# Attention in two places of a two-layer block: each pair's transpose is issued one iteration after its scores, where it was two

## The chip, the cores and the metric

The kernel runs on one core of a Trainium2 chip. The metric is the device time of one execution in microseconds (us). The kernel before was timed in three executions.

## The reference, cut to what matters

The reference runs a first layer (a Hyena mixer and a differential attention mixer) and then a second layer with a mixer and a mixture of experts. The change concerns only the second layer's mixer, which holds two attentions over 512 positions in blocks of 128 queries, all in float32:

```
def dsa_attention(q, k, v, qi, ki, wi):          # 8 heads, one shared key and value
    score = einsum('bth,bths->bts', wi, relu(einsum('bthd,bsd->bths', qi, ki)))
    _, sel = lax.top_k(where(causal, score, -inf), k_sel)     # 128 keys of each query
    s = einsum('bthd,btkd->bthk', q, k[sel]) * scale
    out = einsum('bthk,btkd->bthd', masked_softmax(s, sel <= qpos), v[sel])

def nsa_attention(...):                          # 8 heads in 2 groups
    o_cmp = attention over compressed keys       # blocks of 32 positions
    o_slc = attention over selected blocks       # softmax(q k^T) v
    o_win = attention over a window
    o = gc * o_cmp + gs * o_slc + gw * o_win     # gates per query and head

merged = sigmoid(gate_a) * (o_a @ w_br_a) + sigmoid(gate_b) * (o_b @ w_br_b)
```

The kernel computes the whole causal score row and masks it, so the work of a query block i (0 to 3) is over 128*(i+1) keys.

## The kernel before, in words

The program is written by hand, one instruction list for each engine, with semaphores between them: `tensor`, `scalar`, `vector`, `gpsimd` and `sync` each call their part of each stage in the same order of stages. An engine works its own list strictly in the written order. Nothing but that order decides what stands behind what.

Attention is cut into *pairs*, numbered in the table `PAIRS` (L2869). A pair is one query block with two heads, r = 0 and 1. Pairs 0 to 15 are the first attention, called DSA here (kind "a": query blocks 0 to 3, four pairs each). Pairs 16 to 47 are the second, called NSA here (kinds "slc" and "win", eight pairs for each query block). A *quad* c is the pairs 2c and 2c+1, whose products with the values are made together. The steps of a pair n are:

- `tensor_scores` on TensorE: six matmuls (L3007, L3008) and two that add a mask (L3015), into one of two sets of PSUM banks.
- `vector_scores` on VectorE: two maxima over a row (L3023).
- `scalar_scores` on ScalarE: two exponentials with their row sums (L114), into the buffers R and X of the pair's parity.
- `vector_weigh` on VectorE: the reciprocal of the sums (L3050). For NSA it also multiplies by the gates (L3055) and scales both tiles (L119). For DSA `scalar_weigh` scales them on ScalarE (L114).
- `tensor_turn` on TensorE: i+1 transposes (L3085) for each r, into banks 4 and 5. It waits for the scaled tile and for the previous pair's reads of these banks.
- `scalar_turn` on ScalarE: the high part of the transposed tile (`hi_part`, L98). `vector_turn` on VectorE: the low part (`lo_part`, L102). Both go to tiles called pt_a0h, pt_a0l and so on.
- `tensor_product` on TensorE, once for each quad: 6*(i+1) matmuls (L92 to L94) with the values. For "slc" quads `tensor_compressed_out` adds six matmuls twice. `vector_out` copies the result out (L3145) for all but the "slc" quads, whose result goes on in the same bank.

Between the steps of pair n each engine calls `between(n)`. On TensorE this is `tensor_gate`: matmuls of the projections for `gate_a` and `gate_b`, which need nothing of the attention. They are 12 matmuls of 512 columns for each pair of DSA and 6 for each pair of NSA. On ScalarE it is the conversion of weight chunks (`whi`, L98) and the eviction of the gate results (`gslot`, L114); on GpSimd the gate result is multiplied (L2959); on VectorE it is the low part of weight chunks (`wlo`, L102) and, in DSA, three rounds of `vector_choose` for each pair (L2731, L2733), the selection of the 128 keys, until all are found. The first `between` of NSA (n = 16) also ends the compressed attention's last block (`cT_last`), and `tensor_turn(16)` waits for it.

Each engine's loop is one of the functions `tensor_attend`, `scalar_attend` and `vector_attend`. In the kernel before they have three stages: in iteration n the engine works on the scores of pair n, on the scaling of pair n-1 and on the transpose of pair n-2. The product of a quad stands at the end of the odd iteration n = 2c+3.

## Time and profile before

| | us |
|---|---|
| median of 3 executions | 2574.6 |
| lowest and highest | 2572.97, 2575.89 |
| profiled execution: its own time | 2575.89 |
| profiled execution: span of the trace | 2574.1 |
| PE busy (matmuls) | 2363.1 (92%) |
| DVE busy (VectorE) | 1676.8 (65%) |
| ACT busy (ScalarE) | 1305.7 (51%) |
| POOL busy (GpSimd) | 800.1 (31%) |

The span is the time from the first to the last instruction in the trace; the profiled execution's own time is 1.8 us longer. PE is TensorE's matmuls, PEld its weight loads, DVE is VectorE, ACT is ScalarE, POOL is GpSimd. Matmuls overlap each other, so that a row of a matmul shows a longer time than the step to the next one: steps are read from start to start. Of the span, DSA is the stretch from 1655.7 to 1762.2 us and NSA the stretch from 1855.8 to 2018.7 us. In the profile's 40 slices these are roughly slices 26 to 28 and 29 to 32.

### The profile page before, as it was taken

Reading aid. Unit: us, or ns where it says so; the run is one execution under the profiler, and the core shown is the slowest. Engines: PE = TensorE matmul, PEld = TensorE weight load, DVE = VectorE, ACT = ScalarE, POOL = GpSimd, SP = SyncE. Lnnn points to the kernel's source line nnn. Section 1 sums busy time; section 2 is a strip of 40 time slices with the busy share of each in tenths; the row PEclk is TensorE's granted clock in tenths of the full one; section 3 lists DMA queues with packets and bytes.
Section 4 is the critical chain, followed back from the end, with each engine's and each line's share of the span. In section 5 each row is a group of like instructions: output and inputs, shape, how many; then the busy total and the mean of one; then the engine's idle time right before and its main releaser. Section 6 shows DMA issues by size and latency. Waiting matters only on the chain.

```text
span 2574.1 us, 38547 instructions
## 1 busy us (share of the span) xinstructions
PE 2363.1 (92%) x15891; PEld 2092.4 (81%) x15891; DVE 1676.8 (65%) x2609; ACT 1305.7 (51%) x2147; POOL 800.1 (31%) x496
## 2 busy tenths in 40 slices
PE   8999996989899899999999898888898996999997
PEld 7999996888899889988998677667776775878875
DVE  4454545878843766666656667884576546888885
ACT  4444433444432555555555534354254325888885
POOL 2112123454531122232232022122210023776773
PEclk9999997999999999999999899998898997999999
DMA  5333321011043122222222142123211434878874
GB/s 177 92 90 99 117 62 50 18 33 34 13 134 87 47 78 73 81 67 71 71 75 58 50 110 82 54 54 100 82 50 29 135 109 173 293 279 294 285 263 172
DMA packets 226056, 272.88 MB, mean 106 GB/s; under 512 B 41544, under 2 KB 194089, under 8 KB 213210
## 3 DMA queue, kind: packets, MB, share of 16 engines
q1 hardware_dynamic: 211626, 262.00, 32.6%
q0 software_dynamic: 14256, 8.44, 1.1%
q8 instruction: 125, 2.05, 0.3%
q14 instruction: 49, 0.40, 0.1%
HBM read 282.74 MB, written 31.00 MB: 122 GB/s over the span
## 4 chain that ended last, share of the span: by engine, by line
PE 57%; DVE 20%; ACT 10%; POOL 6%; issue 5%; DMA 2%; SPq 0%; DVEq 0%; POOLq 0%; ACTq 0%
PE ps L92 17%; PE ps L93 16%; PE ps L94 16%; ACT whi L98 2%; DVE wlo L102 2%; DVE prods L1163 2%; PE ps L1839 2%; DVE fsum L990 1%; ACT sp L114 1%; POOL wlo L102 1%; DVE p L2134 1%; POOL xg L3987 1%; PE ps L1849 1%; DVE work L2733 1%; POOL yd L3993 1%
## 5 line engine op out<-in xcount | busy, mean ns | idle before, releaser
L92 PE MATMUL ps<-hn_h,whi 128*128 128x264 f32 (+2 forms) x2256 | 689.9, 306 | 23.7 <-POOL wlo L102 10.3
L94 PE MATMUL ps<-hn_h,wlo 128*128 128x264 f32 (+2 forms) x2256 | 670.1, 297 | 0.0
L93 PE MATMUL ps<-hn_l,whi 128*128 128x264 f32 (+2 forms) x2256 | 670.0, 297 | 0.0
L92 PEld LDWEIGHTS ps<-hn_h,whi 128*128 128x128 f32 x2256 | 428.9, 190 | 52.9 <-issue 17.1
L94 PEld LDWEIGHTS ps<-hn_h,wlo 128*128 128x128 f32 x2256 | 427.9, 190 | 11.6
L93 PEld LDWEIGHTS ps<-hn_l,whi 128*128 128x128 f32 x2256 | 429.7, 190 | 8.9 <-issue 0.2
L102 POOL TENSOR_TENSOR wlo<-wraw,whi 128x2048 fp32r<-128x2048 f32 (+1 forms) x45 | 163.1, 3624 | 540.6 <-ACT whi L98 540.6
L98 ACT ACTIVATE whi<-wraw 128x2048 fp32r<-128x2048 f32 (+1 forms) x164 | 260.4, 1588 | 52.7 <-PE ps L94 44.1
L102 DVE TENSOR_TENSOR wlo<-wraw,whi 128x2048 fp32r<-128x2048 f32 (+1 forms) x119 | 247.2, 2077 | 54.4 <-ACT whi L98 54.3
L750 DVE SCALAR_TENSOR_TENSOR c<-ub,vec,c 128x528 f32<-128x528 f32 x48 | 45.6, 950 | 128.5 <-ACT c L114 128.5
L114 ACT ACTIVATE ub<-ps,vec 128x528 f32<-128x528 f32 x48 | 33.7, 702 | 151.3 <-PE ps L94 151.3
L2184 POOL TENSOR_TENSOR sp<-sp,sp 128x512 f32<-128x512 f32 x16 | 23.5, 1469 | 237.4 <-DMA sp<-sp 237.4
L114 ACT ACTIVATE p<-ps,stat 128x528 f32<-128x528 f32 x64 | 45.0, 703 | 98.3 <-DVE stat L2120 98.2
L3993 POOL DMA_INDIRECT yd<-ys,dst x39 | 84.0, 2153 | 17.2 <-issue 7.7
L3987 POOL DMA_INDIRECT xg<-hnd,tok x39 | 73.7, 1890 | 45.3 <-DVE xe L3960 33.8
L2120 DVE TENSOR_REDUCE stat<-ps 128x1 f32<-128x528 f32 x128 | 83.4, 690 | 1.2 <-PE ps L1839 1.1
L2959 POOL TENSOR_TENSOR gslot<-gslot,rr 128x512 f32<-128x512 f32 x16 | 21.2, 1324 | 198.4 <-ACT gslot L114 198.4
L102 DVE TENSOR_TENSOR ex_lo<-wraw,ex_hi 128x2048 fp32r<-128x2048 f32 x30 | 75.6, 2519 | 9.0 <-ACT ex_hi L98 7.5
L2134 DVE SCALAR_TENSOR_TENSOR p<-p,stat,sp 128x528 f32<-128x528 f32 x60 | 49.4, 824 | 47.7 <-ACT sp L114 47.7
L98 ACT ACTIVATE Y_h<-rr 128x512 fp32r<-128x512 f32 (+1 forms) x40 | 25.3, 632 | 101.1 <-DVE rr L1170 101.1
L92 PE MATMUL ps<-yh,whi 128*128 128x272 f32 (+1 forms) x256 | 73.8, 288 | 2.4 <-POOL yl L102 2.4
L93 PE MATMUL ps<-yl,whi 128*128 128x272 f32 (+1 forms) x256 | 73.5, 287 | 0.0
(786 smaller groups left out, 6704.4 us busy)
## 6 DMA issues: line engine op xcount, KB each, us to landing
wraw<-in_w_gate_up SPq DMA_DIRECT2D x33, 1024.0 KB
wraw<-in_hy_w_in SPq DMA_DIRECT2D x32, 1024.0 KB, 5.7
wraw<-in_da_w_in SPq DMA_DIRECT2D x64, 512.0 KB, 4.3
ex_raw<-in_w_gate_up SPq DMA_DIRECT2D x31, 1024.0 KB
ex_raw<-in_w_down SPq DMA_DIRECT2D x17, 1024.0 KB
wraw<-in_w_down SPq DMA_DIRECT2D x15, 1024.0 KB
wraw<-in_w_in SPq DMA_DIRECT2D x14, 1024.0 KB, 5.4
wraw<-in_hy_w_out SPq DMA_DIRECT2D x8, 1024.0 KB, 7.3
```

What stands on the lines that cost most here:

```text
L92: e.matmul(out, lhsT=l[0], rhs=r[0], start=start, stop=False)
L93: e.matmul(out, lhsT=l[0], rhs=r[1], start=False, stop=False)
L94: return e.matmul(out, lhsT=l[1], rhs=r[0], start=False, stop=stop)
L98: return e.activation(hi, src, ACT.Copy, bias=0.0, scale=scale)
L102: return e.tensor_tensor(lo, src, hi.bitcast(F32), ALU.subtract)
L114: return e.activation(out, in_, func, bias=bias, scale=scale, accum_out=accum)
L1163: e.tensor_tensor(prods[0:n], X.unsqueeze(2).broadcast_to([n, 2, 2, 256]), H.unsqueeze(1).broadcast_to([n, 2, 2, 256]), ALU.mult).then_inc ...
L1839: t = e.matmul(sc[m][:, y, 0:264], lhsT=qk[l][c, q], rhs=qk[r][c, ks], start=(l + r == 0), stop=(l == 1))
L2120: e.tensor_reduce(mx[:, m:m + 1], sc[m][:, :, 0:264], AX.XY, ALU.max, negate=True).then_inc(*mark("da.vec", "max", h, i, m))
L2134: e.scalar_tensor_tensor(p[0][:], p[0][:], ls[:, 0:1], p[1][:], ALU.mult, ALU.add).then_inc(*mark("da.vec", "p", h, i))
L3987: e.indirect_dma_start(xg[n % 4][:], None, hnd, bass.IndirectOffsetOnAxis(tok[:, SLOTS[n]:SLOTS[n] + 1], 0), bounds_check=L - 1, oob_is_er ...
L3993: e.indirect_dma_start(yd, bass.IndirectOffsetOnAxis(dst[:, SLOTS[n]:SLOTS[n] + 1], 0), ys[n % 2][:], None, bounds_check=2 * L - 1, oob_is ...
```

## The change

The three loops get two stages instead of three. TensorE's iteration n now begins with the transpose of pair n-1, then come the scores of pair n and the gate matmuls; the product of a quad stands at the end of the even iteration n = 2c+2. ScalarE's iteration begins with the high parts of pair n-1, then the exponentials of pair n, and for DSA the scaling of the same pair n. VectorE's begins with the low parts of pair n-1, then the maxima, the copy out and the scaling of pair n. No instruction is added or removed, no buffer and no wait's meaning changes.

```diff
     def quad_of(n, a):
 
-        return (n - 3) // 2 if n % 2 and n - 3 >= a else None
+        return n // 2 - 1 if n % 2 == 0 and n > a else None
 
     def tensor_attend(e, w, a, b, between):
-        for n in range(a, b + 2):
+        for n in range(a, b + 1):
             c = quad_of(n, a)
             selected = c is not None and PAIRS[2 * c][0] == "slc"
             if selected:
                 tensor_compressed_out(e, w, c, PAIRS[2 * c][2])
+            if n > a:
+                tensor_turn(e, w, n - 1)
             if n < b:
                 tensor_scores(e, w, n)
-            if n >= a + 2:
-                tensor_turn(e, w, n - 2)
-            if n < b:
                 between(e, w, n)
             if selected:
                 tensor_compressed_out(e, w, c, PAIRS[2 * c][2] + 1)
@@
     def scalar_attend(e, w, a, b, between):
-        for n in range(a, b + 2):
-            if a < n <= b and PAIRS[n - 1][0] == "a":
-                scalar_weigh(e, w, n - 1)
-            if n >= a + 2:
-                scalar_turn(e, w, n - 2)
+        for n in range(a, b + 1):
+            if n > a:
+                scalar_turn(e, w, n - 1)
             if n < b:
                 scalar_scores(e, w, n)
+                if PAIRS[n][0] == "a":
+                    scalar_weigh(e, w, n)
                 between(e, w, n)
 
     def vector_attend(e, w, a, b, between):
-        for n in range(a, b + 3):
+        for n in range(a, b + 2):
             if a < n <= b:
-                vector_weigh(e, w, n - 1)
+                vector_turn(e, w, n - 1)
             if n < b:
                 vector_scores(e, w, n)
-            if a <= n - 2 < b:
-                vector_turn(e, w, n - 2)
             c = quad_of(n - 1, a)
             if c is not None and PAIRS[2 * c][0] != "slc":
                 vector_out(e, w, c)
             if n < b:
+                vector_weigh(e, w, n)
                 between(e, w, n)
```

The order of the instructions is shown at three places. First, TensorE at the start of NSA, before the change. L92 to L94 with hn_h and hn_l are gate matmuls, L3007, L3008 and L3015 the scores of a pair, L3085 a pair's transposes; R_216 and R_217 are the scaled tiles of pair 16:

```order
L94 MATMUL ps<-hn_h,wlo_56 128x512
L3007 MATMUL ps<-kwin_255,qb_h 128x128
L3008 MATMUL ps<-kwin_255,qb_h 128x128
L3007 MATMUL ps<-kwin_256,qb_h 128x128
L3008 MATMUL ps<-kwin_256,qb_h 128x128
L3007 MATMUL ps<-kwin_255,qb_l 128x128
L3008 MATMUL ps<-kwin_255,qb_l 128x128
L3015 MATMUL ps<-trir,identr 128x128 x2
L3085 MATMUL ps<-ident,R_216 128x128
L3085 MATMUL ps<-ident,R_217 128x128
L92 MATMUL ps<-hn_h,whi_54 128x512
```

The same place after the change; L3391 is the transpose of the compressed attention's last block:

```order
L94 MATMUL ps<-hn_h,wlo_56 128x512
L3391 MATMUL ps<-ident,cx 128x128 x2
L3085 MATMUL ps<-ident,R_216 128x128
L3085 MATMUL ps<-ident,R_217 128x128
L3007 MATMUL ps<-kslc_251,qb_h 128x128
L3008 MATMUL ps<-kslc_251,qb_h 128x128
L3007 MATMUL ps<-kslc_252,qb_h 128x128
L3008 MATMUL ps<-kslc_252,qb_h 128x128
L3007 MATMUL ps<-kslc_251,qb_l 128x128
L3008 MATMUL ps<-kslc_251,qb_l 128x128
L3015 MATMUL ps<-trir,identr 128x128 x2
L92 MATMUL ps<-hn_h,whi_54 128x512
```

Pair 16's transposes stood behind the scores of pairs 17 and 18 and the gate matmuls between them; now they stand ahead of the scores of pair 17, right behind pair 16's own gate matmuls.

Second, VectorE at the same place, before the change:

```order
L3023 TENSOR_REDUCE sm<-ps 128x1 x2
L102 TENSOR_TENSOR wlo_55<-wraw_51,whi_53 128x2048
L102 TENSOR_TENSOR cT_last<-ps,cT_last 128x256
L3050 RECIPROCAL sm<-sm 128x2
L3055 TENSOR_TENSOR sm<-sm,gates 128x2
L119 TENSOR_SCALAR R_216<-R_216,sm 128x128
L119 TENSOR_SCALAR R_217<-R_217,sm 128x128
L3023 TENSOR_REDUCE sm<-ps 128x1 x2
```

And after it (pt_b0l and pt_b1l are the low parts of pair 16):

```order
L3023 TENSOR_REDUCE sm<-ps 128x1 x2
L3050 RECIPROCAL sm<-sm 128x2
L3055 TENSOR_TENSOR sm<-sm,gates 128x2
L119 TENSOR_SCALAR R_216<-R_216,sm 128x128
L119 TENSOR_SCALAR R_217<-R_217,sm 128x128
L102 TENSOR_TENSOR wlo_55<-wraw_51,whi_53 128x2048
L102 TENSOR_TENSOR cT_last<-ps,cT_last 128x256
L102 TENSOR_TENSOR pt_b0l<-ps,pt_b0h 128x128
L102 TENSOR_TENSOR pt_b1l<-ps,pt_b1h 128x128
L3023 TENSOR_REDUCE sm<-ps 128x1 x2
L3050 RECIPROCAL sm<-sm 128x2
```

The scaling of a pair now follows the maxima of the same pair with nothing between them, and the low parts of a pair stand ahead of the next pair's maxima.

Third, ScalarE at the start of DSA, as a difference (R and X are the tiles of even and odd pairs; the rows with sm among the outputs are exponentials, those that write R or X alone are the scaling):

```order
 L114 ACTIVATE R_216,sm<-ps,sm 128x128
 L114 ACTIVATE R_217,sm<-ps,sm 128x128
-L98 ACTIVATE whi_54<-wraw_52 128x2048
 L114 ACTIVATE R_216<-R_216,sm 128x128
 L114 ACTIVATE R_217<-R_217,sm 128x128
+L98 ACTIVATE whi_54<-wraw_52 128x2048
+L98 ACTIVATE pt_a0h<-ps 128x128
+L98 ACTIVATE pt_a1h<-ps 128x128
 L114 ACTIVATE X_218,sm<-ps,sm 128x128
 L114 ACTIVATE X_219,sm<-ps,sm 128x128
```

The scaling moved ahead of the weight chunk's conversion, and pair 0's high parts ahead of pair 1's exponentials.

## Rows read from the trace of the kernel before

**Rows 1.** Stretches: length, busy us of each engine, PE clock, DMA share, GB/s.

```profile
1655.70:1762.20 106.50, 92.96 (x524) 73.44 (x524) 82.23 (x202) 59.55 (x149) 23.97 (x11) 0.95 0.18 50
1855.80:2018.70 162.90, 145.53 (x947) 114.31 (x946) 110.05 (x284) 74.08 (x214) 15.44 (x9) 0.92 0.11 33
1695.80:1726.77 30.97, 23.60 (x132) 18.54 (x130) 28.35 (x64) 15.19 (x37) 7.90 (x4) 0.95 0.20 55
```

**Rows 2.** Waits of PE in NSA: us in total, times, longest.

```profile
PE ps L92 <- DVE pt_b2l L102: 9.0, 5, 4.2
PE ps L92 <- DVE obT L3145: 5.3, 6, 2.1
```

**Rows 3.** The same for DSA.

```profile
PE ps L92 <- DVE pt_a2l L102: 7.5, 4, 3.5
```

**Rows 4.** Timeline, two iterations of NSA's query block 3: start, us, engine, line.

```profile
1987.23 0.50 PE L3007 MATMUL ps<-kslc,qb_h 64*128 64x512 f32 x1
...
1988.41 1.06 PE L3085 MATMUL ps<-ident,R 128*128 128x128 f32 x8
1988.51 1.29 DVE L3023 TENSOR_REDUCE sm<-ps 128x1 f32<-128x512 f32 x2 [1.61 <-PE ps L3015]
...
1989.57 0.59 ACT L98 ACTIVATE pt_b3h<-ps 128x512 fp32r<-128x512 f32 x1
...
1990.32 0.68 DVE L102 TENSOR_TENSOR pt_b3l<-ps,pt_b3h 128x512 fp32r<-128x512 f32 x1
...
1990.80 0.49 PE L3007 MATMUL ps<-kslc,qb_h 64*128 64x512 f32 x1
...
1997.54 0.50 PE L3007 MATMUL ps<-kwin,qb_h 64*128 64x512 f32 x1
```

**Rows 5.** Timeline, VectorE from maxima to scaling, query block 3.

```profile
1968.67 1.28 DVE L3023 TENSOR_REDUCE sm<-ps 128x1 f32<-128x512 f32 x2
...
1970.87 0.17 DVE L3050 RECIPROCAL sm<-sm 128x2 f32<-128x2 f32 x1
...
1971.27 0.88 DVE L119 TENSOR_SCALAR X<-X,sm 128x512 f32<-128x512 f32 x2
```

**Rows 6.** The same for query block 0.

```profile
1867.01 0.48 DVE L3023 TENSOR_REDUCE sm<-ps 128x1 f32<-128x128 f32 x2
...
1868.17 0.17 DVE L3050 RECIPROCAL sm<-sm 128x2 f32<-128x2 f32 x1 [0.28 <-ACT R L114]
...
1868.57 0.48 DVE L119 TENSOR_SCALAR R<-R,sm 128x128 f32<-128x128 f32 x2
```

**Rows 7.** Timeline, an iteration of query block 0 without product.

```profile
1871.16 0.32 PE L3007 MATMUL ps<-kslc,qb_h 64*128 64x128 f32 x1
...
1873.65 0.32 PE L3007 MATMUL ps<-kslc,qb_h 64*128 64x128 f32 x1
...
1874.49 0.49 DVE L3023 TENSOR_REDUCE sm<-ps 128x1 f32<-128x128 f32 x2 [0.18 <-PE ps L3015]
```

**Rows 8.** Timeline, start of NSA.

```profile
1861.73 2.29 DVE L102 TENSOR_TENSOR wlo<-wraw,whi 128x2048 fp32r<-128x2048 f32 x1 [2.48 <-ACT whi L98]
1863.94 0.42 DVE L102 TENSOR_TENSOR cT_last<-ps,cT_last 128x256 fp32r<-128x256 f32 x1
...
1864.66 0.48 DVE L119 TENSOR_SCALAR R<-R,sm 128x128 f32<-128x128 f32 x2
1865.00 0.53 PE L3085 MATMUL ps<-ident,R 128*128 128x128 f32 x2 [1.51 <-DVE R L119]
```

**Rows 9.** Stretch that holds one compressed output of six matmuls.

```profile
1912.97:1913.48 0.51, 0.51 (x6) 0.43 (x6) 0.44 (x3) 0.00 (x0) 0.00 (x0) 1.00 0.00 0
```

**Rows 10.** Timeline, a scaling beside GpSimd's multiplication.

```profile
1984.97 1.92 DVE L119 TENSOR_SCALAR X<-X,sm 128x512 f32<-128x512 f32 x2
1985.11 1.50 POOL L2959 TENSOR_TENSOR gslot<-gslot,rr 128x512 f32<-128x512 f32 x1 [25.95 <-ACT gslot L114]
```

**Rows 11.** Stretches of the same form: iterations 35 and 39 of NSA.

```profile
1932.04:1940.81 8.77, 8.77 (x47) 7.00 (x46) 3.76 (x10) 2.71 (x7) 1.29 (x1) 0.62 0.00 0
1953.62:1959.49 5.87, 5.87 (x46) 4.83 (x44) 4.74 (x10) 2.48 (x7) 1.43 (x1) 1.00 0.00 0
```

## The prediction, made before the changed kernel ran

> **What bounds the kernel now.** I first read the busy shares and the 40 slices of the page: TensorE is busy 92% of the span, so time is won or lost where it stands still or runs at a lower clock. Then I cut out the two stretches that the change touches. In DSA TensorE is busy 92.96 of 106.5 us at a mean granted clock of 0.95, in NSA 145.53 of 162.9 us at 0.92 [rows 1]. So 13.5 and 17.4 us stand idle there, 30.9 us in all, and that is all that a better order alone could give back.
>
> The waits of TensorE say what it stands for. In NSA 9.0 us are waits of a product for the low parts of its transposed tile and 5.3 us are waits of a compressed output for the copy out of the bank before it [rows 2]; 1.5 us more are the first transpose of the stage [rows 8]. In DSA the largest entry is again a product that waits for low parts, 7.5 us in 4 waits [rows 3], but there VectorE itself is full: in four iterations, 1695.8 to 1726.8, it is busy 28.35 of 30.97 us while TensorE is busy 23.60 [rows 1]. The selection rounds make it so. So DSA is bound by VectorE until the selection ends (about two thirds of it), and NSA by TensorE with stalls.
>
> Last I followed one iteration on all engines, to learn how long a pair needs from its scores to its transpose, because that is the time which the old order hid behind a whole iteration and the new one doesn't.
>
> **The change part by part.**
>
> *The new chain.* In the new order iteration n+1 begins with the transposes of pair n. Everything between two such starts must happen in a row: transposes of n-1, high and low parts, maxima of n, exponentials, sums, scaling. TensorE meanwhile has the scores and the gate matmuls of one iteration and, at even n, a product. Behind the waiting transpose are queued the next scores and gate matmuls, all of TensorE's work.
>
> Query block 3 (512 keys). From the start of the transposes (1988.41) the second high part ends at 1990.16, 1.75 later; the second low part takes 0.68 [rows 4]. I take 2.45 to the first maximum: the low parts now stand ahead of it. From the first maximum to the reciprocal it is 1970.87 - 1968.67 = 2.20, from there to the scaling 0.40 [rows 5]. The first of two scalings is done after half of 0.88, and 0.10 for the signal: 0.54. Sum 2.45 + 2.20 + 0.40 + 0.54 = 5.59.
>
> Query block 0 (128 keys). The maximum follows the scores' start by 1874.49 - 1873.65 = 0.84 [rows 7]; the two transposes ahead of the scores are 0.32 by my estimate (the eight of rows 4 step by about 0.12 each, and a change-over). From the maximum to the reciprocal 1.16, to the scaling 0.40 [rows 6]; from the scaling to the first transpose 1865.00 - 1864.66 = 0.34 [rows 8]. Sum 3.06.
>
> TensorE's own work in an iteration without product is 1990.80 - 1987.23 = 3.57 for block 3 [rows 4] and 1873.65 - 1871.16 = 2.49 for block 0 [rows 7]. So an odd iteration now leaves a hole of 5.59 - 3.57 = 2.02, or 3.06 - 2.49 = 0.57. Blocks 1 and 2 lie between; the mean is 1.30, and NSA has 16 odd iterations: 20.7 us. After half of them a compressed output of 0.51 [rows 9] stands ahead of the transpose and fills part of the hole: 8 x 0.51 = 4.1. That leaves 16.6.
>
> Even iterations have the product: 1997.54 - 1990.80 = 6.74, less a wait of 0.25, is 6.5 for block 3 [rows 4], more than 5.59. Nothing is exposed there, and the product finds its low parts, which are done 2.45 after the transposes' start.
>
> *Further waits in NSA.* A scaling that meets GpSimd's multiplication takes 1.92 instead of 0.88 [rows 5, 10]. Now it stands in the chain. There are 8 gate results, all in odd iterations; for block 0 the gate's eviction comes too late to meet the scaling, so 6 x 0.9 = 5.4. The bounds are 0 (it falls elsewhere) and 8 x 1.04 = 8.3. The low part of a weight chunk on VectorE takes 2.29 [rows 8] and now stands between a pair's scaling and its low parts: two of them inside the stage, 1.5 each after the slack of their even iteration, 3.0 (bounds 0 and 4.6). The start: the transpose of pair 16 waits for `cT_last`, which ends at 1864.36 [rows 8] as before. But in the old order TensorE had done two scores and one gate block (2.49 and 0.8) before its wait of 1.51; those stand behind the wait now. It has run out at 1865.00 - 1.51 - 3.3 = 1860.2, and waits 4.1. The last product waits for its low parts, 2.45 less the transposes' 0.9: 1.5. Sum of the new waits: 16.6 + 5.4 + 3.0 + 4.1 + 1.5 = 30.6 us.
>
> *What goes.* The 17.4 us of idle time in NSA: the product waits and the waits for the copy out, since low parts and copy now stand ahead of the scaling. Net for NSA: +13.2.
>
> *DSA.* A pair's scaling is on ScalarE, but VectorE waits for the exponentials before it goes on to the selection: from maximum to reciprocal 1.16 to 2.20, less the 0.4 to 1.3 that the two maxima take themselves, is 0.7 to 0.9 in each iteration [rows 4 to 6]. Over the 12 or so with selection that is 10 us at most. Against it stand the waits of VectorE for high parts, which go (2.6 us in four iterations, 8 in twelve [rows 1]), and the copy out, which falls into every second new wait. So -8 to +10; I take +2, near the middle, since VectorE's work is the same and its idle time of one kind is replaced by another of about the same size. The product waits of 13.5 us vanish by name and come back as waits for scores or transposes, because VectorE is what is late. In the last four pairs TensorE's 12 gate matmuls cover the chain but for some 0.5 us twice, and the drain is shorter by about as much.
>
> *The clock.* After the wait of 2.1 us [rows 2], which stood ahead of iteration 35, the granted clock fell: the iteration took 8.77 us at 0.62 where its twin took 5.87 at 1.00 [rows 11], so one such fall costs 2.9. Today three waits of NSA (2 to 4.2 us) are followed by one. The new order has the 4.1 at the start and four or five of 2.5 to 3 (where hole and GpSimd meet). I take one fall more: +3. Bounds: -6 (two fewer, the waits being spread thin) and +25 (below).
>
> The Trainium skill ("TensorE: Matmul & The Clock Gate", HAM oscillation) holds that only an idle gap beyond a certain length throttles the array. By that rule alone most of the new holes are harmless and the clock term would be -3 to 0, the sum some 4 us lower. The trace speaks for more caution: a wait of 2 us stood ahead of the 0.62.
>
> The Trainium skill ("GPSIMD Engine Reference", Specifications) also says that GpSimd shares its SBUF interfaces with VectorE, contended by instructions in a two-port mode or with two SBUF inputs. A scaling from SBUF to SBUF is of the first sort. By the rule all 8 meetings are possible, without it the 5.4 would be 0; the 1.92 beside 0.88 agrees with the rule.
>
> *Sum.* 13.2 + 2 + 3 = 18.2, on the profiled execution's 2575.9 (span 2574.1 and 1.8 around it): 2594.1. That execution was the slowest of three, 1.3 above the median, so against the median the same sum is 2592.8. I say 2594.
>
> **The rivals.**
>
> *The chain is shorter than I make it: no change.* If the two heads overlap better than the rows of single instructions show, the hole is 0.5 instead of 1.3. The new waits are 30.6 - 16 x 0.8 = 17.8, against 17.4 that go; with nothing for DSA and clock the time is 2576. For it: these intervals were measured on engines that were in part busy with other things. Against it: the maximum-to-reciprocal intervals are those of waiting engines, so they can't shrink. It also holds if the waits that go are simply renamed.
>
> *The waits for low parts were the real loss: faster.* VectorE would have to be the bound in NSA too. There it is busy 110 of 163 us [rows 1], so its order matters more than its load. With holes of 0.5 and no meeting with GpSimd (17.8 - 5.4 = 12.4 against 17.4), -8 in DSA, and one fall of the clock less: 2575.9 - 5 - 8 - 3 = 2560. For it: 9.0 + 5.3 + 7.5 us of named waits do go. Against it: gate matmuls of 1.4 us can't cover a chain of 3.1 to 5.6.
>
> *The clock stays down.* With a hole in every second iteration the granted clock could be at half for long parts of NSA. At 0.92 it is at half for some 26 of 163 us; if for half of 180 us, that is 64 us more. Rows 11 give 2.9 us lost for 6.6 at half, so 0.44 each, 28 in all, of which a fifth hides in the holes: 22. The time is 2594 + 22 = 2616. For it: the 0.62 after 2 us. Against it: most holes are below 2 us and DSA has waits of 3.5 that cost little.
>
> **How the numbers follow.** Forecast (chain exposed, clock about as now): chance 0.66, its own range +6 to +30, from holes of 0.9 to 1.6 (6 either way), meetings 0 to 8, DSA. Clock down: 0.14. No change: 0.12. Faster: 0.08. The range is 2577 to 2614: it leaves out the faster case and the worse half of the clock case. About 5 us either way (0.2%) can't be told from no change here. Faster by more than that 0.07, within it 0.11, slower 0.82.
>
> **What would show it.** In the profile after: the waits of L3085 on L119 should be the largest entry of TensorE in NSA, in odd iterations, growing from 0.6 to 2 us with the query block; the waits of L92 on low parts and on obT should be almost gone; the first transpose of NSA should wait about 4 us; NSA should be some 176 us long and DSA 105 to 112. TensorE's busy time there should hardly change. I am wrong if the transposes wait little, if DSA's length changes by more than 8 us, or if the mean clock in NSA leaves 0.88 to 0.96.

## The result, and the profile after

| | before | after |
|---|---|---|
| median of 4 executions each, us | 2575.24 | 2600.28 |
| lowest and highest | 2572.97, 2586.09 | 2598.05, 2602.09 |
| span of the profiled execution | 2574.1 | 2597.1 |

The changed kernel is slower: the ratio to before is 1.009, with a 95% interval of 1.0065 to 1.0114. Three more executions of the changed kernel (2594.88, 2603.32 and 2604.82 us) count in that ratio; the medians alone differ by 25.0 us. The profile accounts for 23.0 us between the two spans. The stretches of DSA and NSA in the changed kernel, with the columns of [rows 1]:

```profile
1662.20:1771.00 108.80, 94.62 (x524) 71.91 (x524) 82.00 (x202) 61.04 (x149) 24.07 (x11) 0.97 0.18 49
1863.90:2043.60 179.70, 154.20 (x947) 117.44 (x946) 108.61 (x283) 77.74 (x214) 15.60 (x9) 0.90 0.10 30
```

NSA is 16.8 us longer and DSA 2.3 longer than in [rows 1]. The program ahead of DSA took 6.6 us more (1662.3 against 1655.7), what lies between and behind took 2.7 us less in all. The 6.6 us are in code that the change doesn't touch, and a later run of the kernel before shows them too (below). In NSA TensorE stands idle for 179.7 - 154.20 = 25.5 us, 8.1 more than before; the other 8.7 us are in its busy time, with the same 947 groups of matmuls, at a mean clock of 0.90 after 0.92.

The waits of TensorE in NSA, then in DSA (us in total, times, longest), which answer to [rows 2] and [rows 3]; obT is the tile that the product is copied out to:

```profile
PE ps L3085 <- DVE X L119: 14.8, 18, 1.9
PE ps L92 <- DVE obT L3145: 5.8, 5, 2.4
PE ps L3085 <- DVE cT_last L102: 4.1, 1, 4.1
```

```profile
PE ps L3085 <- ACT X L114: 10.1, 7, 2.3
PE ps L3085 <- ACT R L114: 2.1, 3, 1.0
```

The product's waits for low parts are gone from NSA (9.0 before). In their place the transposes wait for the scaled tile X, which is the tile of the odd pairs: it is the scaling of the very pair that is to be turned. In DSA the same wait has taken over. The first transpose of NSA, against 1.51 in [rows 8]:

```profile
1872.60 0.66 PE L3085 MATMUL ps<-ident,R 128*128 128x128 f32 x2 [4.07 <-DVE cT_last L102]
```

The loop is seen in one iteration of query block 3 (start, us, engine, line; in brackets the idle time before and who ended it):

```profile
2004.38 1.03 PE L3085 MATMUL ps<-ident,R 128*128 128x128 f32 x8
...
2005.65 0.69 DVE L102 TENSOR_TENSOR pt_b2l<-ps,pt_b2h 128x512 fp32r<-128x512 f32 x1 [2.28 <-ACT pt_b2h L98]
...
2006.86 1.28 DVE L3023 TENSOR_REDUCE sm<-ps 128x1 f32<-128x512 f32 x2
...
2009.06 0.17 DVE L3050 RECIPROCAL sm<-sm 128x2 f32<-128x2 f32 x1 [0.92 <-ACT X L114]
...
2009.45 1.89 DVE L119 TENSOR_SCALAR X<-X,sm 128x512 f32<-128x512 f32 x2
2009.59 1.48 POOL L2959 TENSOR_TENSOR gslot<-gslot,rr 128x512 f32<-128x512 f32 x1 [24.93 <-ACT gslot L114]
...
2009.99 1.02 PE L3085 MATMUL ps<-ident,X 128*128 128x128 f32 x4 [1.85 <-DVE X L119]
```

From one start of transposes to the next it is 2009.99 - 2004.38 = 5.61 us. The maxima of 2006.86 wait for two things that both begin with the transposes of 2004.38: the low parts, which end on VectorE about there, and their own scores, which TensorE makes behind the transposes and ends at 2006.68. The odd iterations without a compressed output in the other blocks show waits of 0.38 in block 0, 0.8 in block 1 and 1.36 in block 2, where block 3 has 1.85.

The granted clock in NSA (column PEclk, third from the end):

```profile
1863.90:1878.00 14.10, 10.03 (x41) 7.29 (x40) 7.99 (x24) 4.60 (x13) 0.00 (x0) 0.53 0.00 1
1878.00:1907.00 29.00, 26.16 (x172) 19.50 (x170) 17.65 (x65) 14.37 (x52) 2.56 (x2) 1.00 0.17 55
1907.00:1918.00 11.00, 10.46 (x48) 8.24 (x48) 3.87 (x13) 2.50 (x9) 0.00 (x0) 0.53 0.01 1
...
1959.00:1967.00 8.00, 5.86 (x28) 4.49 (x29) 5.21 (x12) 3.67 (x10) 1.41 (x1) 0.79 0.01 3
...
1984.00:1992.00 8.00, 7.21 (x41) 5.82 (x40) 5.58 (x10) 4.76 (x8) 0.65 (x1) 0.79 0.01 3
...
2009.00:2018.00 9.00, 7.61 (x30) 5.53 (x31) 6.08 (x12) 3.67 (x9) 1.48 (x1) 0.62 0.01 2
```

Five stretches have time at half clock: the start, one behind a wait of 2.37 us for a copy (ended at 1907.42), and three behind an odd iteration in which TensorE waited 1.36 to 1.85 us for X and again for the second tile, whose scaling met GpSimd's multiplication. A like pair of waits at 2038.06 (1.84 and 0.75 us) has no low stretch behind it within NSA, so such a wait doesn't always bring one. The kernel before has five as well (1855.8 to 1860, 1893 to 1897, 1932 to 1938, 1970 to 1977 and 2013 to 2017). What differs is the sum. With the stretch of NSA cut where the granted clock changes, the four profiles of the two orders give:

| | half clock in NSA, us | TensorE busy in it, us |
|---|---|---|
| before | 24.8 | 23.7 |
| before, profiled again (below) | 27.3 | 23.7 |
| changed | 37.0 | 32.5 |
| the new order in NSA alone (below) | 40.5 | 35.4 |

### The profile page after: what moved, and what is told of

It reads as the page before. It is cut to its first block, busy times and chain, and to the rows that moved or that the text cites. A ratio compares the mean times of both kernels' runs of the same rounds, so it can differ in the third digit from the quotient of the medians.

```text
span 2597.1 us, 38538 instructions
## 1 busy us (share of the span) xinstructions
PE 2377.0 (92%) x15891; PEld 2098.4 (81%) x15891; DVE 1678.1 (65%) x2609; ACT 1311.1 (50%) x2147; POOL 801.1 (31%) x496
## 4 chain that ended last, share of the span: by engine, by line
PE 56%; DVE 22%; ACT 11%; POOL 6%; issue 4%; DMA 2%; SPq 0%; DVEq 0%; POOLq 0%; ACTq 0%
PE ps L92 17%; PE ps L93 15%; PE ps L94 15%; DVE prods L1163 2%; PE ps L1839 2%; ACT whi L98 2%; DVE wlo L102 1%; DVE fsum L990 1%; ACT sp L114 1%; DVE work L2733 1%; DVE m L2731 1%; DVE p L2134 1%; PE ps L1849 1%; ACT X L114 1%; POOL wlo L102 1%
## 5 line engine op out<-in xcount | busy, mean ns | idle before, releaser
L92 PE MATMUL ps<-hn_h,whi 128*128 128x264 f32 (+2 forms) x2256 | 688.8, 305 | 24.9 <-POOL wlo L102 10.0
L94 PE MATMUL ps<-hn_h,wlo 128*128 128x264 f32 (+2 forms) x2256 | 670.7, 297 | 0.0
L92 PEld LDWEIGHTS ps<-hn_h,whi 128*128 128x128 f32 x2256 | 429.8, 191 | 54.8 <-issue 18.5
L94 PEld LDWEIGHTS ps<-hn_h,wlo 128*128 128x128 f32 x2256 | 428.5, 190 | 11.8
L92 PE MATMUL ps<-yh,whi 128*128 128x272 f32 (+1 forms) x256 | 73.8, 288 | 2.4 <-POOL yl L102 2.4
L94 PE MATMUL ps<-yh,wlo 128*128 128x272 f32 (+1 forms) x256 | 73.5, 287 | 0.0
```

The lines of the kernel that those rows point to most:

```text
L92: e.matmul(out, lhsT=l[0], rhs=r[0], start=start, stop=False)
L94: return e.matmul(out, lhsT=l[1], rhs=r[0], start=False, stop=stop)
```

## The experiments

The runs of a group shared a chip and the runs of the kernel before: medians of 2578.9 us (23 executions) for the first four, 2579.8 (18) for the next four, 2579.9 (29) for the last four. There the kernel before varies by more than it did here (2569 to 2592 in the first), so ratios with their intervals are what counts. Where a length is given, it is read from one profiled execution of the run.

### Each attention alone, and the kernel before again

Two copies of the three loops, one in the old and one in the new order; DSA calls one and NSA the other.

```diff
-        tensor_attend(e, w, 0, 16, tensor_gate)
+        tensor_attend_n(e, w, 0, 16, tensor_gate)     # DSA new
-        tensor_attend(e, w, 16, 48, tensor_gate)
+        tensor_attend_o(e, w, 16, 48, tensor_gate)    # NSA old; the other run: o and n swapped
```

> Two stages in DSA only, NSA keeps its three. Theory (the loss is the chain exposed in NSA, DSA is bound by VectorE either way): DSA about 2 us longer than before (106 to 108), NSA as before (162), the whole +0 to +5 us. Rival (the stages cost in both places alike, about 1 us a hole): DSA has 8 odd iterations, so +6 to +9. Second rival (what stands ahead of DSA also grows, by 6.6 us, because the program is another one): the stretch ahead of DSA is 1662 us instead of 1656 here too, and the whole +7 to +9.

> Two stages in NSA only, DSA keeps its three. Theory: NSA 176 to 180 us instead of 162, of it about 8 us more idle time of TensorE and 8 us more busy time at the lower clock; the whole +15 to +20. Rival (DSA's order matters as much): less than +12. Second rival (another program shifts what stands ahead by 6.6): +22 to +26.

> The kernel before, unchanged, profiled again. If the 6.6 us by which the stretch ahead of DSA was longer in the changed kernel's profile are chance, this profile's stretch lies anywhere between 1654 and 1663 us and its whole is within 5 us of the kernel before. If they belong to the program, the stretch is 1655 to 1657 us again.

The new order in DSA alone: ratio 1.0014 (0.9995 to 1.0034). In NSA alone: 1.0081 (1.0055 to 1.0106). The kernel before again: 0.999 (0.9975 to 1.0006). So nearly all of the loss is NSA's. NSA's 182.8 us with the new order alone lie above the 176 to 180 that the expectation gave, DSA's 108.8 a little above its 106 to 108. DSA and NSA of the first, then of the second, then the program ahead of DSA and NSA in the third:

```profile
1662.60:1771.40 108.80, 94.60 (x524) 72.08 (x524) 82.01 (x202) 60.87 (x149) 24.02 (x11) 0.97 0.18 49
1864.40:2025.40 161.00, 145.17 (x947) 114.11 (x946) 110.16 (x283) 74.01 (x214) 15.59 (x9) 0.93 0.11 33
```

```profile
1655.00:1759.10 104.10, 92.22 (x524) 72.40 (x524) 82.22 (x202) 59.48 (x149) 23.96 (x11) 0.95 0.18 51
1853.20:2036.00 182.80, 155.47 (x947) 118.36 (x946) 108.79 (x283) 77.68 (x214) 15.59 (x9) 0.89 0.10 30
```

```profile
0.00:1664.20 1664.20, 1539.63 (x11729) 1436.89 (x11729) 1031.38 (x1601) 773.02 (x1325) 437.07 (x332) 0.97 0.26 74
1862.30:2023.30 161.00, 145.21 (x947) 114.12 (x946) 110.14 (x283) 73.91 (x214) 15.58 (x9) 0.92 0.11 33
```

With identical code the program ahead of DSA took 1664.2 us here and 1655.7 in the first execution, so the 6.6 us of the result are not the change's. The old order's DSA took 104.1 us in this run and in the second, against 106.5 in [rows 1]; the new order's took 108.8 in each of the two. The DSA term is then 2.3 to 4.7 us in the profiles, and too small to be told in the times. The old order's NSA was 161.0 us long in the first and the third run, after 162.9, and the new order's 182.8 after 179.7, so NSA's part of the loss is 16.8 to 21.8 us by the profiles.

### The start of NSA

The compressed attention's last block goes ahead of the weight chunk in the first `between` of NSA, on ScalarE and on VectorE. The rest is the changed kernel.

```diff
         def between(e, w, n):
-            lo_gate(e, w, "vec", n)
             if n == 16:
                 vector_compressed(e, w, 3, 1)
+            lo_gate(e, w, "vec", n)
```

> The changed kernel, but in the first iteration of NSA the compressed attention's last block is finished ahead of the weight chunk, on ScalarE and VectorE, so that the transposes of pair 16 need not wait for that chunk. Theory: the first wait falls from 4.1 to under 1.5 us; NSA 176 instead of 179, the whole 2 to 4 us below the changed kernel (+21 over before). Rival (the long first wait also holds the clock down behind it, and that is the larger part): 5 to 9 us below the changed kernel, mean clock of NSA 0.92 or more.

The ratio to before is 1.0063 (1.0038 to 1.0088); the interval overlaps the changed kernel's. The wait went as meant, the clock didn't come (the waits of the whole of NSA, then its first 16 us):

```profile
PE ps L3085 <- DVE cT_last L102: 1.0, 1, 1.0
```

```profile
1863.80:1880.00 16.20, 15.05 (x56) 10.76 (x56) 9.68 (x32) 5.84 (x19) 0.00 (x0) 0.50 0.01 2
```

The wait fell from 4.1 to 1.0 us, but TensorE ran at 0.50 for the whole first 16 us, where the changed kernel has 0.59 over the same stretch. NSA was 182.7 us long, where 176 was expected; the profiled execution was the slowest of its six (2602.21 us, median 2595.09), and by the ratio the edit may have won a few us that the intervals can't separate from nothing. A shorter wait doesn't bring the clock up by itself.

Nor does the long stretch at half clock belong to the new order. The kernel before, profiled again, has 13.7 us of it at the start of NSA, with TensorE busy throughout; the changed kernel has 13.1:

```profile
1862.30:1876.00 13.70, 13.70 (x53) 10.25 (x52) 8.88 (x30) 5.40 (x17) 0.00 (x0) 0.50 0.00 0
```

In its first profile only the first 4.2 us were at 0.50, and yet NSA was no shorter there (162.9 against 161.0); the wait of 1.51 us of [rows 8] is missing from the second, where TensorE comes to that transpose at the lower clock. With the old order the half clock at the start of NSA thus lasted 4.2 us in one execution and 13.7 in another.

### The order within an iteration

Both keep the new depth: the transpose one iteration behind the scores. The first swaps two steps on TensorE alone, the second swaps two on VectorE also, in both attentions.

```diff
     def tensor_attend(e, w, a, b, between):
+            if n < b:
+                tensor_scores(e, w, n)
             if n > a:
                 tensor_turn(e, w, n - 1)
             if n < b:
-                tensor_scores(e, w, n)
                 between(e, w, n)
```
```diff
     def vector_attend(e, w, a, b, between):
-            if a < n <= b:
-                vector_turn(e, w, n - 1)
             if n < b:
                 vector_scores(e, w, n)
+            if a < n <= b:
+                vector_turn(e, w, n - 1)
```

> The changed kernel, but on TensorE alone the scores of pair n stand ahead of the transposes of pair n-1 (both attentions). Theory (the loss is a loop through VectorE: transposes, low parts, maxima, exponentials, scaling, transposes; the maxima of n stand behind the low parts of n-1, so the loop keeps its length): the waits for the scaling stay within 3 us of 14.8 us, and of NSA's 179.7 us only the first wait gets shorter by about 1.5; the whole within 6 us of the changed kernel. Rival (the loss is only that the scores stand behind the waiting transposes on TensorE): the holes shrink by the 1.0 us of a pair's scores each, NSA 165 us or less, the whole 12 us or more below the changed kernel.

> As the run before it, and on VectorE also the maxima of pair n ahead of the low parts of pair n-1. Theory: this cuts the loop to maxima, exponentials, scaling, which is 0.1 + 2.2 + 0.4 + 0.5 = 3.2 us for query block 3 and less than TensorE's 3.6 us; the waits for the scaling fall from 14.8 to 5 us or less, NSA 158 to 166 us, and DSA, where the low parts now fill the wait for the exponentials, 100 to 107 us instead of 108.8; the whole between -8 and +3 us against the kernel before. Rival (the low parts then come too late for the product, and the waits move there, as in the kernel before): waits of L92 on low parts 8 us or more, NSA 170 or more.

TensorE's swap alone: ratio 1.013 (1.0108 to 1.0152), worse than the changed kernel by some 10 us, where the expectation was within 6. Both swaps: 0.9994 (0.9981 to 1.0008), the whole loss gone. The waits in NSA, one fence for each, and the second one's stretch of NSA:

```profile
PE ps L3085 <- DVE X L119: 16.0, 16, 3.2
PE ps L92 <- DVE obT L3145: 13.2, 7, 3.4
```

```profile
PE ps L92 <- DVE obT L3145: 7.7, 6, 2.7
PE ps L3085 <- DVE X L119: 6.2, 8, 1.6
```

```profile
1857.80:2020.90 163.10, 145.07 (x947) 113.56 (x946) 108.72 (x284) 74.47 (x214) 15.66 (x9) 0.93 0.11 33
```

The second of these runs settles the cause. The depth is not what costs: with the same depth NSA takes 163.1 us, as before (162.9 and 161.0), and no product of NSA waits for low parts. What costs is that the old pair's transposes stand ahead of the new scores on TensorE, and its low parts ahead of the new maxima on VectorE, so that nothing of the new pair begins before the old one is through, while the next transposes wait for the new pair. TensorE's swap alone leaves that chain closed: NSA went to 189.2 us. Where a compressed output waits for the copy, the scores now stand between it and the transposes:

```profile
1995.48 1.06 PE L3085 MATMUL ps<-ident,R 128*128 128x128 f32 x8
...
2000.23 0.27 PE L92 MATMUL ps<-cT_last,vc_h 32*64 32x128 f32 x1 [2.28 <-DVE obT L3145]
...
2001.90 1.44 PE L3085 MATMUL ps<-ident,X 128*128 128x128 f32 x8
```

From transposes to transposes that is 6.42 us; the same place took 1997.36 - 1991.62 = 5.74 in the changed kernel. The theory had X's waits right (16.0) and missed that the wait for the copy would grow to 13.2. VectorE's swap alone was not run, so that it needs both is shown from one side only.

The maxima of the second run start when their scores are there, ahead of the low parts:

```profile
2009.92 1.29 DVE L3023 TENSOR_REDUCE sm<-ps 128x1 f32<-128x512 f32 x2 [2.64 <-PE ps L3015]
2011.13 0.69 DVE L102 TENSOR_TENSOR pt_b2l<-ps,pt_b2h 128x512 fp32r<-128x512 f32 x1
...
2012.95 0.17 DVE L3050 RECIPROCAL sm<-sm 128x2 f32<-128x2 f32 x1 [0.54 <-ACT X L114]
```

The low parts now lie where VectorE would wait for the exponentials: its wait ahead of the reciprocal is 0.54 us there, after 0.92 in the changed kernel. The waits for X are 6.2 us where 5 or less were expected; of these 4.0 stand ahead of a second tile, whose scaling met GpSimd's multiplication.

### The scaling and GpSimd's multiplication

In the changed kernel the scaling of NSA works on 4 columns instead of all, which leaves the rest unscaled; and in another run GpSimd multiplies 16 of 512 columns of a gate result, which leaves the rest unmultiplied.

```diff
-                ts(e, p, p, f[:, r:r + 1], None, ALU.mult)...
+                ts(e, p[:, 0:4], p[:, 0:4], f[:, r:r + 1], None, ALU.mult)...
```
```diff
-                e.tensor_tensor(gslot[:], gslot[:], rr2[:], ALU.mult)...
+                e.tensor_tensor(gslot[:, 0:16], gslot[:, 0:16], rr2[:, 0:16], ALU.mult)...
```

> The changed kernel, but in NSA VectorE scales only four columns of each tile, so the result leaves the scaling out. Theory (every part of the chain is paid for at the holes): the scaling's 0.5 to 0.9 us go from each hole, the waits for it fall from 14.8 to 6 us or less, NSA 160 to 168 us. Rival (the holes don't add up to the loss, the clock does, and it falls as often): NSA 173 or more at a mean clock of 0.90 or less.

> The changed kernel, but GpSimd multiplies only 16 of 512 columns of each gate result, so the result leaves the rest out. Theory (a scaling that meets GpSimd's multiplication takes 1 us longer, and it is these longest holes after which the clock falls): the waits for the scaling fall by 4 to 6 us, the falls of the clock go from five to two or three, NSA 168 to 173 us. Rival (the clock falls by chance of the moment, not by the length of a hole): the waits fall the same, the clock's mean stays 0.88 to 0.91, NSA 174 to 177 us.

Ratios 1.0048 (1.0028 to 1.0068) and 1.0059 (1.0037 to 1.0082). Without the scaling NSA was 173.2 us long, where 160 to 168 was expected, TensorE's waits for X were 11.1 us where at most 6 was, and for the copy 7.5: the theory that scaling is the heavy link is missed. In block 3 the wait went from 1.85 to 1.61 only, since the other links of the chain remain. What did stay is the meeting. VectorE with 4 columns twice, and GpSimd beside it:

```profile
1957.88 1.42 DVE L119 TENSOR_SCALAR X<-X,sm 128x4 f32<-128x4 f32 x2
```

```profile
1958.02 1.26 POOL L2959 TENSOR_TENSOR gslot<-gslot,rr 128x512 f32<-128x512 f32 x1 [12.19 <-ACT gslot L114]
```

VectorE's pair of tiny instructions, which takes 0.36 elsewhere in this run, ends at 1959.30 and GpSimd's multiplication at 1959.28. With the small multiplication VectorE loses nothing, its 0.75 being the time without a meeting, and GpSimd takes 0.36 where it has 0.22 when it meets nothing:

```profile
1962.95 0.75 DVE L119 TENSOR_SCALAR X<-X,sm 128x384 f32<-128x384 f32 x2
```

```profile
1963.08 0.36 POOL L2959 TENSOR_TENSOR gslot<-gslot,rr 128x16 f32<-128x16 f32 x1 [12.38 <-ACT gslot L114]
```

The waits for X fell from 14.8 to 11.1 us, and the transposes of blocks 2 and 3 that had taken 1.9 to 2.5 us took 0.9 to 1.2. But NSA was 178.8 us long at a clock of 0.89, where the theory said 168 to 173: a wait of 2.4 us for the copy stood at 1995.8, where the changed kernel had 0.95, and the clock was 0.66 over the 10 us behind it. That wait is not the edit's doing. It was 2.38 us too in the other two profiles of the new order, with NSA alone and with the start mended; in the changed kernel's own profile TensorE ran at half clock from 1986.3 to 1989.7 and came there later. By its length the run speaks for neither side.

### The copy out ahead of the maxima

With both swaps the largest wait left is the compressed output's for the copy (7.7 us). Three kernels move that copy, in NSA only, to the front of VectorE's iteration: the one with both swaps, the changed one, and the kernel before. A fourth adds the edit at the start of NSA to the first of these.

```diff
     def vector_attend(e, w, a, b, between):
         for n in ...:
+            c = quad_of(n - 1, a)
+            if c is not None and PAIRS[2 * c][0] == "win":
+                vector_out(e, w, c)
 ...
-            c = quad_of(n - 1, a)
-            if c is not None and PAIRS[2 * c][0] != "slc":
+            if c is not None and PAIRS[2 * c][0] == "a":
                 vector_out(e, w, c)
```

> The order of the run before it (scores ahead of the transposes of the pair before, maxima ahead of its low parts), and in NSA the copy out of a product's bank (L3145, 0.86 us) moved to the front of VectorE's iteration, ahead of the maxima. Theory: with that order TensorE's largest named wait in NSA is the compressed output's for the copy, 7.7 us in 6 waits up to 2.7, only because the copy stands behind two maxima and two low parts. Put first it falls where VectorE waits for scores anyway (32 us in 22 waits). Waits for obT at most 2 us, waits of L3085 on L119 not above 9 (6.2), NSA 157 to 161 us (163.1), the whole 3 to 8 us below the kernel before. Rival: the hole belongs to the weight chunk's low part of 2.29 us on VectorE, so the same time comes back as waits of L3085 on L119 of 11 us or more, NSA 162 to 166, the whole within 3 us of the kernel before.

> The run above with the end of the compressed attention (cT_last) ahead of the weight chunk in the first iteration of NSA, on ScalarE and VectorE. Theory: the first transposes' wait goes from 3.3 us to under 1 and TensorE's clock, at half over the first 16 us or so in all runs, is no lower than there; NSA 2 to 3 us shorter than in the run above. Rival, from the same edit in the changed kernel: the wait goes but the granted clock stays at 0.50 to 0.55 for longer (over 14 us), what is won is given back, NSA within 1.5 us of the run above or longer.

> The changed kernel with only the copy out moved to the front of VectorE's iteration in NSA. Theory: the copy is a link of the chain from one transpose to the next (low parts, maxima, copy, scaling), in half of the odd iterations. Moved ahead it lies where VectorE waits for the high parts (37 us), and those holes shrink by up to 0.9 us each: waits for obT (5.8 us in 5) go, waits of L3085 on L119 grow by at most 3 (14.8), idle time of NSA 20 to 22 us (25.5). With the fall of the clock after the wait of 2.4 us gone, NSA is 171 to 176 us (179.7), and the whole 4 to 8 us below the changed kernel, still 10 to 18 above the kernel before. Rival: the copy costs the chain nothing, the waits are only renamed: L3085 on L119 19 us or more, NSA 178 to 181, the whole within 3 us of the changed kernel.

> The kernel before with only the copy out moved to the front of VectorE's iteration in NSA. Theory: its waits for obT (5.3 us in 6, up to 2.1) go; the scaling behind the copy has a whole iteration of slack, so nothing new is late; waits of the product for low parts 7 to 11 us (9.0), NSA 157 to 161 (162.9), the whole 2 to 6 us below the kernel before. Rival: the copy first waits for the end of the product and keeps the scaling and the low parts behind it, so the product waits longer for low parts: pt_b2l 12 us or more, NSA 164 to 168, the whole 1 to 6 us above.

| | median, us | ratio to before | NSA, us |
|---|---|---|---|
| both swaps, copy first | 2575.34 | 0.9977 (0.9961 to 0.9994) | 159.0 |
| the same, and the start | 2570.66 | 0.9959 (0.9946 to 0.9972) | 155.3 |
| changed kernel, copy first | 2600.10 | 1.0077 (1.0053 to 1.0101) | 182.8 |
| before, copy first | 2572.10 | 0.9976 (0.996 to 0.9992) | 155.6 |

The stretch of NSA of the second of these and its waits:

```profile
1854.60:2009.90 155.30, 140.95 (x947) 110.33 (x946) 109.62 (x284) 74.43 (x214) 15.50 (x9) 0.97 0.11 35
```

```profile
PE ps L3085 <- DVE X L119: 11.9, 12, 1.9
PE ps L92 <- DVE obT L3145: 1.4, 1, 1.4
PE ps L3085 <- DVE cT_last L102: 0.4, 1, 0.4
```

It is the fastest kernel of the study, 0.4% below before, and has the highest mean clock in NSA, 0.97, though its waits for X are longer than the 10.0 us of the first. Its interval overlaps those of the other two that gain, so which of its edits carries how much isn't told.

In the changed kernel the same edit won nothing: the rival was right. Its waits:

```profile
PE ps L3085 <- DVE X L119: 24.0, 21, 2.8
PE ps L3085 <- DVE cT_last L102: 4.1, 1, 4.1
PE ps L92 <- DVE obT L3145: 1.0, 1, 1.0
```

The waits for the copy came back under the transposes' name. The two entries are 25.0 us together for 20.6; most of the rest came at two places behind a weight chunk (3.4 for 2.4 us, and 2.8 for 1.4). The second of these is no rise: it is the place that had 2.38 + 0.41 = 2.79 us in both other profiles of the changed order in NSA. Against the 22.6 us of the run with the new order in NSA alone, 2.4 came anew: 0.9 at the first place, 0.9 from a meeting with GpSimd in block 1 that it doesn't have, and 0.4 at another place of that block. At one place of block 3 the changed kernel waits 0.83 for the copy and 0.46 for X behind it; with the copy first there is one wait:

```profile
2024.41 0.27 PE L92 MATMUL ps<-cT_last,vc_h 32*64 32x128 f32 x1 [0.83 <-DVE obT L3145]
...
2025.44 1.09 PE L3085 MATMUL ps<-ident,X 128*128 128x128 f32 x8 [0.46 <-DVE X L119]
```

```profile
2027.63 1.09 PE L3085 MATMUL ps<-ident,X 128*128 128x128 f32 x8 [1.37 <-DVE X L119]
```

0.83 + 0.46 = 1.29 is 1.37 under another name. The other three gained about what their theories said (ratios in the table): NSA was shorter than foreseen in the kernel before with the copy first (155.6 for 157 to 161) and with the start mended (3.7 us less for 2 to 3), and the waits for X a little above the 9 us set for the first (10.0). In the kernel before, where a scaling has a whole iteration of slack, the copy's waits (5.3 us) vanished and nothing took their place.

## Why the prediction was right

It said 2594 us and slower with a chance of 0.82; the median is 2600.3. By the ratio the change costs some 23 us (17 to 29), the forecast was 18, its own range 6 to 30. Direction and mechanism hold. For NSA it said 16.2 us (13.2 and 3), and the profiles show 16.8 to 21.8. That fit is in part luck: the idle time was set 5.1 us too high and the busy time 5.7 too low, and the two nearly cancel.

- **The chain in the odd iterations.** Right, and shown by the run with both swaps, which opens the chain at the same depth and loses nothing. The length came out at 5.61 us in block 3, where 5.59 was worked out, and at 1884.67 - 1881.61 = 3.06 in block 0, as worked out. The holes were a little smaller, 1.85 for 2.02 and 0.38 for 0.57, because TensorE's own work was longer: 5.61 - 1.85 = 3.76, not 3.57.
- **The compressed output as filling.** Right in size: in blocks 2 and 3 a hole with it is 0.79 (0.47 + 0.32) and 1.29 us, and one without 1.36 and 1.85, so it fills 0.57 (0.51 was taken). Wrong was the step that the waits for the copy out go because the copy now stands ahead of the scaling: 5.8 us of TensorE's waits bear its name. The copy stands behind the maxima of the same iteration, so TensorE's next instruction waits for it first and then for X. As the run with the copy first in the changed kernel shows, it is the same hole, and nearly no time of its own.
- **Weight chunks.** 3.0 us predicted, from two low parts on VectorE at 1.5 each. The first made the hole at 1907.4, 2.37 us where the block's holes of that kind would be 0.8 - 0.57 = 0.23. The second, at 1990.8, cost about 0.1 in this profile (0.95 + 0.45 = 1.40 for 1.29) and 1.5 in the other two of this order. A third place was not foreseen: the hole at 1948 is 1.21 + 0.89 = 2.10 where 0.79 is due. There ScalarE's conversion of a chunk made the high parts 0.8 us late, and VectorE's small multiplication by the gates took 0.73 us where 0.16 is usual, until GpSimd's own low part of a chunk was over (rows below). Together some 3.6 us more, for 3.0: the size is right in part by luck.

```profile
1944.60 4.56 POOL L102 TENSOR_TENSOR wlo<-wraw,whi 128x2048 fp32r<-128x2048 f32 x1 [5.37 <-ACT whi L98]
...
1948.44 0.73 DVE L3055 TENSOR_TENSOR sm<-sm,gates 128x2 f32<-128x2 f32 x1
```

- **The start of NSA.** 4.1 us predicted, 4.07 measured.
- **GpSimd.** Six meetings at 0.9 were predicted. Five times a pair's transposes took about 1.0 us longer because the second tile came late (1.4 at 2009.99, at half clock); so 5 us for 5.4. Of this some 3.6 us show as waits (20.6 us of waits for X and the copy, less 17.0 ahead of a first transpose or compressed output). The rest stands in the busy time, since the first tile's last transpose counts in full where otherwise the next one begins under it. The small multiplication took it away.
- **The last product.** 1.5 us predicted, none found: the meeting delays the second tile's transposes, and the first tile's low part is done by then. In the run with the small multiplication, which has no such delay, the wait is there, 0.97 us.
- **Sum of the idle time.** 30.6 us of new waits predicted, 24.7 found (14.8, 5.8 and 4.1), within an idle time of 25.5. Net +8.1 for +13.2; 1.4 of the missing 5.1 stands in the busy time (5 us of meetings less 3.6).
- **The clock and the busy time.** It said that TensorE's busy time "should hardly change"; that rose by 8.7 us. Of TensorE's busy time 8.8 us more stood at half clock (32.5 for 23.7), which is worth at most half of that, 4.4 us, and 5.9 in the other profile (35.4). I take this as the clock's part: 4 to 6 us, an estimate, where 3 were taken. The meetings explain 1.4. Some 3 us remain, and no run separates them; part is that a matmul row ahead of a hole counts in full, 0.40 us where the step to the next is 0.23, and NSA has 24 waits where it had 13. It is not the long stretch at half clock at the start, since the kernel before shows one of 13.7 us as well. The mean of 0.90 lies within the 0.88 to 0.96 that were named. The Trainium skill ("TensorE: Matmul & The Clock Gate", HAM oscillation) warns of idle gaps beyond a certain length, which throttle the array. The trace goes further: low stretches stand behind shorter waits too, of 2.37 us, and of 1.36 us with one of 0.80 after it.
- **DSA.** +2 predicted, +2.3 between the two profiles, and up to +4.7 against later profiles of the old order. The waits came back as waits of the transposes for the scaled tiles, as said. The 13.5 us that the prediction calls product waits there are DSA's whole idle time; the waits for low parts are 7.5 [rows 3].

The rival "the chain is shorter" needed holes of 0.5 us and is refuted by the rows of blocks 1 to 3. "The waits for low parts were the real loss" fails with NSA's longer idle time. "The clock stays down" had its 22 us from half of NSA at half clock; at a mean of 0.90 it is about a fifth.

Open remains what sets the length of the half clock at the start of NSA. Over the first 16 us the mean was 0.50 with the start mended in the changed kernel and 0.78 with the same edit in the kernel with both swaps and the copy first. Since the kernel before alone gave 4.2 us in one execution and 13.7 in another, a single profile of each can't lay that on the order.

## What to carry to other kernels

The depth of a software pipeline says little by itself: look for the cycle that the in-order queues close over an iteration. Here transposes, low parts, maxima, exponentials and scaling stood in a ring because each engine finished the old pair before it began the new one; swapping two steps on two engines, new pair first, opened it, and swapping on TensorE alone made it worse. A wait's name tells who came last, not what to shorten: the same move of the copy won 0.2% where the copy alone was late and nothing where a longer chain ended at the same moment.

## What the runs showed of the hardware

Two VectorE scalings on 4 columns each took 0.36 us together alone, and 1.42 beside a GpSimd multiplication of 1.26 us, ending 0.02 us after it. Two of 384 columns took 0.75 alone and 1.76 beside one of 1.41; two of 512 columns 0.88 and 1.89. So a meeting cost VectorE 1.0 to 1.1 us whatever its own length, and nothing beside a multiplication of 0.36 us (0.75 again). VectorE's multiplication of two tiles of 128x2 waited likewise, 0.73 for 0.16 us, and ended 0.01 us after GpSimd's instruction; the low parts that ran beside the same instruction, with one input in PSUM, took their usual 0.56. The Trainium skill ("GPSIMD Engine Reference", Specifications) has the two engines share their interfaces to SBUF, and these rows agree.

The clock at the start of one and the same stage of one and the same program was at half for 4.2 us in one execution and for 13.7 in another, in the second with TensorE busy all the time.

The spread between executions of the kernel before was 3 us in the first three and 23 us on the chip of the first experiments (2569.33 to 2591.97 over 23), so that a term of 2 to 5 us, such as DSA's, was read from profiles and couldn't be confirmed by times.
